# A pad of 192 bytes instead of 64 between the normed inputs and the weight buffers

## What is computed

```
h    = modulate(rmsnorm(x), shift, scale)          # conditioned norm
proj = h @ w_in                                    # 2048 -> 3904 (first block), 14416 (second)
...attention of two kinds on slices of proj...
x   += gate * (mix @ w_out)                        # 2048 -> 2048
h    = modulate(rmsnorm(x), shift_f, scale_f)
f    = square(relu(h @ w_ff1)) @ w_ff2             # 2048 -> 8192 -> 2048
x   += gate_f * f
```

## The kernel before, in words

| tensor | start behind `acts`, modulo 1024 | modulo 256 | modulo 128 |
|---|---|---|---|
| `acts` | 0 | 0 | 0 |
| `raw`, `hi`, `lo`, `ada_ring`, `cross` | 64 | 64 | 64 |
| `work`, `proj`, `f_acts` | 256 | 0 | 0 |

## Time and profile before

### The profile page before, as it was taken

How to read it: one execution, slowest core, us unless ns; L and a number is a source line. 1 busy time by engine, 2 the same in 40 slices (tenths; PEclk the granted TensorE clock), 3 DMA queues, 4 the chain that set the end, 5 groups by cost and what they waited for, 6 DMA issues and landing times.

```text
span 2836.6 us, 54544 instructions
## 1 busy us (share of the span) xinstructions
PE 2707.4 (95%) x21752; PEld 2561.8 (90%) x21752; DVE 1941.1 (68%) x2021; ACT 1111.1 (39%) x1256; POOL 171.9 (6%) x281
## 2 busy tenths in 40 slices
PE   5799999899999999998998999999989999999998
PEld 1486778899999999998998999999989999999997
DVE  1446686787787875777877878788756566575655
ACT  2234443443343442433333444444334344344433
POOL 5000000110000000010000000000000000000000
PEclk8799999899999998998999999999969999999998
DMA  9887766488888886884765655467727566665653
GB/s 373 331 302 261 239 204 207 165 283 308 289 287 291 284 293 194 285 281 138 248 209 190 228 190 165 153 211 267 268 91 243 202 212 234 200 237 200 227 189 111
DMA packets 299838, 658.71 MB, mean 232 GB/s; under 512 B 30688, under 2 KB 37176, under 8 KB 295224
## 3 DMA queue, kind: packets, MB, share of 16 engines
q1 hardware_dynamic: 267448, 539.35, 55.1%
q0 software_dynamic: 32256, 117.45, 12.7%
HBM read 654.62 MB, written 2.10 MB: 232 GB/s over the span
## 4 chain that ended last, share of the span: by engine, by line
PE 87%; DVE 5%; DMA 4%; ACT 2%; issue 2%; SPq 0%; DVEq 0%; ACTq 0%; POOLq 0%
PE ps L1616 25%; PE ps L1617 24%; PE ps L1618 24%; DMA proj<-in_w_ada 2%; PE ps L1661 2%; PE ps L1663 2%; PE ps L1662 1%; PE ps L1714 1%; PE ps L2041 1%; DVE lo L905 1%; ACT hi L555 1%; PE ps L1779 1%; DMA ada_ring<-in_w_ada 1%; DMA raw<-in_w_ff 1%; DMA raw<-in_w_in 1%
## 5 line engine op out<-in xcount | busy, mean ns | idle before, releaser
L905 DVE TENSOR_TENSOR lo<-raw,hi 128x1024 fp32r<-128x1024 f32 x868 | 1049.5, 1222 | 652.9 <-ACT hi L555 650.9
L555 ACT ACTIVATE hi<-raw 128x1024 fp32r<-128x1024 f32 x868 | 910.7, 1059 | 1339.1 <-PE ps L1618 1081.3
L1616 PE MATMUL ps<-acts,hi 128*128 128x256 f32 x4432 | 1254.6, 283 | 26.7 <-DVE lo L905 15.2
L1617 PE MATMUL ps<-acts,hi 128*128 128x256 f32 x4432 | 1241.5, 280 | 0.0
L1618 PE MATMUL ps<-acts,lo 128*128 128x256 f32 x4432 | 1241.0, 280 | 0.0
L1616 PEld LDWEIGHTS ps<-acts,hi 128*128 128x128 f32 x4432 | 844.3, 191 | 56.4 <-issue 33.3
L1618 PEld LDWEIGHTS ps<-acts,lo 128*128 128x128 f32 x4432 | 846.2, 191 | 0.5
L1617 PEld LDWEIGHTS ps<-acts,hi 128*128 128x128 f32 x4432 | 843.5, 190 | 2.1 <-issue 1.2
L1616 PE MATMUL ps<-f_acts,hi 128*128 128x256 f32 x2048 | 568.2, 277 | 4.8 <-DVE lo L905 4.6
L1618 PE MATMUL ps<-f_acts,lo 128*128 128x256 f32 x2048 | 567.4, 277 | 0.0
L1617 PE MATMUL ps<-f_acts,hi 128*128 128x256 f32 x2048 | 567.4, 277 | 0.0
(11 more groups left out here) (238 smaller groups left out, 1468.6 us busy)
## 6 DMA issues: line engine op xcount, KB each, us to landing
raw<-in_w_ff SPq DMA_DIRECT2D x512, 512.0 KB, 4.7
raw<-in_w_in SPq DMA_DIRECT2D x232, 512.0 KB, 4.7
ada_ring<-in_w_ada POOLq DMA_DIRECT2D x224, 512.0 KB, 5.0
proj<-in_w_ada SPq DMA_DIRECT2D x32, 1024.0 KB, 8.1
ada_ring<-in_w_ada SPq DMA_DIRECT2D x44, 512.0 KB, 4.5
work<-in_w_ada SPq DMA_DIRECT2D x32, 512.0 KB, 4.4
raw<-in_w_out SPq DMA_DIRECT2D x32, 512.0 KB, 4.6
raw<-in_w_o SPq DMA_DIRECT2D x32, 512.0 KB, 5.3
```

What stands on the lines that cost most here:

```text
L555: nc.scalar.activation(hi[n % SPLIT][:, :], raw[n % RAW][:, :], ACT.Copy).then_inc(hi_ready, 1)
L905: V.tensor_tensor(lo[n % SPLIT][:, :], raw[n % RAW][:, :], hi[n % SPLIT][:, :].bitcast(F32), ALU.subtract)\
L1616: M(out, h, right[:, 0:S], start=start, stop=False)
L1617: M(out, h, right[:, S:2 * S], start=False, stop=False)
```

## The change

The pad ahead of the weight buffers is 48 float32 wide instead of 16: 192 bytes instead of 64. Nothing else is changed; the program has the same instructions in the same order. All tensors declared behind the pad move by 128 bytes, and `xT` and `acts` stay. Behind `acts`, modulo 1024, the weight buffers then start at 192 (they were at 64) and `work`, `proj` and `f_acts` at 384 (they were at 256). Modulo 128 nothing changes. Among themselves the moved tensors keep their distances, those of `f_acts` and the weight buffers too.

```diff
         xT = sb("xT", [P, KT, S])
         acts = sb("acts", [P, KT, 2 * S], F32R)
-        sb("weights_shift", [P, 16])
+        sb("weights_shift", [P, 48])
         raw = [sb(f"raw{i}", [P, CHUNK]) for i in range(RAW)]
```

## The result

The changed kernel takes 2891.39 us, the median of 20 runs (2876.56 to 2904.15), against 2863.41 us for the kernel before (20 runs, 2837.64 to 2887.62). The ratio is 1.0125, 95% interval 1.01 to 1.0149: slower. Every ratio in this document is taken from the runs within 1.5% of their kernel's fastest, while medians and spreads are of all runs; the ratio of the two medians is 1.0098. The prediction was no change, 2862.5 us. The measured time lies in its range and in the first rival's, whose mechanism it is.

A forecast was written before the change was run, and what follows sets the result against it. The prediction took TensorE's matmuls of `product` (73% of the span) to bound the kernel. All its terms were 0 us, so the median of 2862.46 gave 2862.5 us, with a range from 2846 to 2893.

The forecast's parts named there:

- the first rival: Period 256 and 192 a bad distance: products on `acts` at 117.7 ns, slower, 2868 to 2907 us; chance 0.21.
- the two rhythms: Product streams on TensorE: tight at 113.3 ns a matmul or loose at about 117.7, 13.3 ns a triple apart.
- instructions, VectorE, ScalarE and their waits: Whole kernel: no instruction or wait changes, and buffer places make no difference over 4 ns on VectorE; 0 us.
- The value projections: 576 matmuls reading `acts` and the weights: bound 2.5 us either way, taken as 0.
- The DMA stage: DMAs into `proj`, first 90 us: moved start gains at most 3% of 70 us, 2 us; taken as 0.
- The estimate after the Trainium skill: DMA packets into `proj`: unaligned start costs 4 beats of 32 bytes in 260, 1.5% or 1 us.
- products on `acts`: 4432 triples, weights' distance going from 64 to 192: period taken as 128, so 0 us; bounds +44.3 and -14.7.
- the half way point: Distance 128 modulo 256 in `ki2`: should be best if only 0 were bad, but isn't, arguing for period 128.
- the term of `f_acts`: Products on `f_acts`: distance to the weights stays, so 2048 triples x 0 = 0 us.
- Rival 3: Products on `acts`: 113.3 ns is itself a conflict that the new distance lifts, 59 us less, 2804 us; chance 0.03.
- The base: Whole kernel: 0 us added to the profiled 2838.37 and to the median 2862.46; differences under 5.7 us count as none.

The follow-up runs named there:

- both_tight: Kernel before plus 128 unused bytes between `hi` and `lo` and 128 ahead of `proj`; 2829.66 us, ratio 0.989.

## Why the prediction was wrong

Its frame held. The bound is the pace of the products; the two rhythms have the paces and the step of 13.3 ns a triple that it read off; instructions, VectorE, ScalarE and their waits gave 0, as it said. The value projections gave +2.4 us, at its bound of 2.5. The DMA stage gave nothing, as far as one trace of each tells. In the window of the earlier trace rows, with `proj` now at a multiple of 256 bytes:

```profile
DMA packets 3977, 28.94 MB, mean 413 GB/s; under 512 B 447, under 2 KB 447, under 8 KB 447
```

The bytes fell by 1% where the bound had allowed 3% more. The estimate after the Trainium skill ("DMA: Bandwidth & Descriptors", section "How a descriptor splits into AXI transactions"), 1.5% more, is not seen either; the page gives the rule for reads, and here `proj` is written.

The step that failed is *products on `acts`*, in its sentence "I take 128, and 0". It ran: 64 and 320 are alike, so the period divides 256; distance 128 in `ki2` is bad; under a period of 256 with one bad place at 0 the half way point should be the best; so 0 and 128 are both bad and the period is 128. Only the first two parts were read from rows. The rest presumed that a pace falls off evenly from one bad place. The map shows nothing of the kind: for long streams 0, 32, 48, 80, 96, 128, 192 and 224 are all bad, by unequal amounts, and of the distances tried 64 alone can be good. At 192 the products on `acts` cost 40.1 us where the prediction had 0. The trace of before held one bad distance and one good one, and from two points a shape was made. Without that shape the rows said only that 192 had never been seen, and that is no ground for 0.62.

`ki2` was also no guide to the long streams. After the change its first half stands at 192 and its second at 0, and it did what the prediction asked for in its own case:

```profile
1525.01 0.28 PE L1618 MATMUL ps<-acts,lo 128*16 128x256 f32 x1
...
1525.71 0.28 PE L1618 MATMUL ps<-acts,lo 128*16 128x256 f32 x1
...
1526.39 0.28 PE L1618 MATMUL ps<-acts,lo 128*16 128x256 f32 x1
```

0.70 us for the second half of a chunk and 0.68 for the first half of the next: in `ki2`, where every other product is 16 wide and the distance changes after six matmuls, 192 is as tight as 64. The start times in nanoseconds also correct a reading. Before the change the second half, at 128, took 693 or 694 ns, 115.6 a matmul and not 116.7; the 0.70 is a rounding. At 0 it takes 700. So even in `ki2` 128 and 0 differ.

The first rival named the right mechanism and the right sign to look for: windows on `acts` at 117.7 ns, those on `f_acts` at 113.3. Its price for a kernel whose `acts` is loose throughout, +44.3 us, was measured at +40.1 between the two traces, for 9018 matmuls instead of 9984: 407 ran at the half clock or beside a pause, 226 of `acts` were still tight after, and 333 of before had been loose in pieces too short for the windows of the earlier trace rows. It missed the term of `f_acts`, put at 2048 triples x 0: 15.2 us there, most of it handed on from `acts`. The timeline had shown that a rhythm outlasts many matmuls, and the groups on `f_acts` follow those on `acts` with no break. That it is kept until the next break, as the prediction has it, is too strong: at 831 us, and in the middle of the group from 653 us, it changed without one.

Rival 3 had 113.3 ns as no floor. In none of these kernels does a long stream go below it. The Trainium skill's isolated gap of the columns' time plus 2.5 ns ("TensorE: Matmul & The Clock Gate", section "Back-to-back issue gap"), 109.2 ns here, is not reached by any of them; with these loads, at every distance tried, the traces are 4.1 ns or more above it.

The base was misjudged too. The three runs of before lay within 1.6 us, and the prediction took a difference of 0.2% to be measurable and the profiled execution's 24 us to be an offset. In truth the program's own executions spread over 50 us, and the profiled one was short because most of its streams happened to be tight. That the measured time still fell inside the stated range is luck in part: the loss between the traces, put on the predicted base, would have ended above it. The loss between the medians, 28 us, is half of that between the traces, 57.9.

What stays open: what the operands meet in. That a load of weights and the moving columns get in each other's way when read at certain distances is argued from the map, not shown. Nor is it known what decides the rhythm after a break at distance 64, why 117.8 ns is handed on to `f_acts` at some borders and not at others and 120 at none, why `ki2` is tight at 192, or why `hi` at 64 with `lo` at 192 has no lasting loose rhythm.

## What to carry to other kernels

When streams of matmuls bound a kernel, divide the length of clean windows by their count, operand by operand, before looking at anything else: the same instruction may run at two paces, and durations hide it. The relative start of stationary and moving buffers, modulo 256 and in steps of 32 bytes or finer, is then worth a scan with unused pads; here the worst and the best layout tried lie 3.3% apart, and the best one was found only because the high and low weights were moved separately. If a program's times spread by 2% from one execution to the next, take some twenty of them and look for such a choice in the trace, and don't infer a shape in an address from two points.

## What was not expected of the hardware

- A stream of identical matmuls (256 columns, fp32r, each with its own 128 x 128 load) has more than one lasting pace at a granted clock of 1.00: 113.3 and 117.8 ns at distance 64, 117.8 and 123.3 at 48, 118.8 and 117.2 at 96.
- A rhythm can survive a change of the moving operand without a pause (117.8 ns from `acts` to `f_acts` at 2230 us) and can be lost at the same border (831 us); one loose stream turned tight in its middle, at a start that came 146 ns behind the last, instead of 117 to 121 (665 us).
- The distance that costs a long stream 4.4 ns a matmul, 192, costs nothing in `ki2`, where six matmuls take 0.68 us.
- Two thirds of the loads at distance 192 and one third at 64 give 118.9 ns, all at 192 give 117.8, one third at 192 and two thirds at 64 give 113.3.
- With 256 unused bytes in the right places the time of the program varied over 8.6 us (six runs of both_tight), and without them over 57.7 us (eleven runs of the kernel before, taken beside it).
